# A state-space scan moved into the delta rule's scan, with batched 64-wide decays, in a one-core Trainium2 layer kernel

## What is computed

```python
def ssd_scan(x, bm, dt, A, s0, cm):            # per direction
    acum = cumsum(dt * A)                      # within a chunk of 64
    a_last = acum[..., -1]
    s_chunk = einsum('bgnsk,bghns,bghnsp->bghnkp', bm, exp(a_last - acum) * dt, x)
    def step(s, inp): sc, al = inp; return s * exp(al) + sc, s
    s_fin, s_starts = scan(step, s0, (s_chunk, a_last))
    seg = exp(where(c >= s, acum[c] - acum[s], -inf)) * dt[s]
    cb = einsum('bgnck,bgnsk->bgncs', cm, bm)
    y = einsum(cb, seg, x) + einsum(cm, s_starts) * exp(acum)
# then: y_f + y_b + D*x, times silu(z), rms_norm per group, joined with the delta output, @ w_out
```

## Time and profile before

| | |
|---|---|
| median of 3 runs | 1584.43 us |
| the profiled execution | 1585.72 us, span 1583.9 us |
| TensorE busy | 1329.1 us (84%) |
| VectorE, ScalarE, GpSimd busy | 505.1, 253.8, 124.0 us |
| DMA | 456.96 MB, mean 289 GB/s |
| stages by the timeline | delta 288.3 to 460.9, ssd 460.9 to 570.0 |

### The profile page before, as it was taken

How to read it: one execution, slowest core, us unless ns; L and a number is a source line. 1 busy time by engine, 2 the same in 40 slices (tenths; PEclk the granted TensorE clock), 3 DMA queues, 4 the chain that set the end, 5 groups by cost and what they waited for, 6 DMA issues and landing times.

```text
span 1583.9 us, 26942 instructions
## 1 busy us (share of the span) xinstructions
PE 1329.1 (84%) x11056; PEld 627.9 (40%) x11057; DVE 505.1 (32%) x1073; ACT 253.8 (16%) x450; POOL 124.0 (8%) x173
## 2 busy tenths in 40 slices
PE   5899899645657937999898898898899999999995
PEld 1746334535545423333333333333243333333332
DVE  0115333472455755232221321221131223232323
ACT  2411421104120131111110110110010001010102
POOL 1101220322115130000000000000000000000000
PEclk9599999755565867999999999999899999999998
DMA  9304255000031056999999999999999879997993
GB/s 369 140 13 138 88 208 205 2 4 4 3 130 38 0 242 275 426 429 427 427 429 427 428 427 429 427 427 427 427 428 427 382 320 428 428 413 300 427 427 144
DMA packets 46946, 456.96 MB, mean 289 GB/s; under 512 B 4227, under 2 KB 4483, under 8 KB 21795
## 3 DMA queue, kind: packets, MB, share of 16 engines
q1 hardware_dynamic: 46886, 456.08, 69.3%
HBM read 455.01 MB, written 1.05 MB: 288 GB/s over the span
## 4 chain that ended last, share of the span: by engine, by line
PE 33%; DMA 26%; DVE 2%; ACT 2%; issue 1%; DVEq 0%; ACTq 0%
DMA arena<-in_w_up 26%; PE bank L999 20%; PE bank L1028 8%; PE bank L971 2%; PE bank L962 2%; ACT arena L1302 1%; PE bank L992 1%; PE bank L1023 0%; DVE arena L1775 0%; ACT arena L1300 0%; DVE arena L1778 0%; ACT L1077 0%; ACT L1075 0%; DVE arena L1919 0%; DVE arena L1769 0%
## 5 line engine op out<-in xcount | busy, mean ns | idle before, releaser
L999 PE MATMUL bank<-arena 128*64 128x512 f32 x2176 | 483.5, 597 | 33.8 <-DMA arena<-in_w_up 19.1
L999 PEld LDWEIGHTS bank<-arena 128*64 128x64 f32 x2176 | 154.9, 137 | 343.7 <-issue 269.6
L1028 PE MATMUL bank<-arena 128*64 128x512 f32 x1088 | 239.4, 592 | 0.0
L1883 DVE TENSOR_SCALAR arena<-bank 128x512 f32<-128x512 f32 x34 | 23.6, 693 | 395.4 <-PE bank L999 395.4
L1028 PEld LDWEIGHTS bank<-arena 128*64 128x64 f32 x1088 | 78.5, 136 | 138.1 <-issue 135.7
L566 PE MATMUL bank<-arena 128*128 128x512 f32 (+1 forms) x320 | 119.0, 528 | 0.0
L1864 DVE TENSOR_TENSOR arena<-arena,bank 128x512 f32<-128x512 f32 x140 | 86.6, 681 | 6.0 <-PE bank L971 6.0
L566 PEld LDWEIGHTS bank<-arena 128*128 128x128 f32 x320 | 60.2, 189 | 55.9 <-issue 53.5
L962 PEld LDWEIGHTS bank<-arena 128*128 128x128 bf16 x1680 | 60.2, 118 | 27.0 <-DVE arena L1887 25.8
L971 PE MATMUL bank<-arena 64*128 64x512 f32 x280 | 69.6, 614 | 0.9 <-ACT arena L1304 0.9
L962 PE MATMUL bank<-arena 128*128 128x64 bf16 x1680 | 64.1, 199 | 1.1 <-DVE arena L1806 1.1
(11 more groups left out here) (331 smaller groups left out, 1226.8 us busy)
## 6 DMA issues: line engine op xcount, KB each, us to landing
arena<-in_w_gate SPq DMA_DIRECT2D x64, 2048.0 KB, 20.2
arena<-in_w_up SPq DMA_DIRECT2D x64, 2048.0 KB, 21.9
arena<-in_w_down SPq DMA_DIRECT2D x64, 2048.0 KB, 21.2
arena<-in_w_ada SPq DMA_DIRECT2D x12, 2048.0 KB, 9.4
arena<-in_wfm SPq DMA_DIRECT2D x20, 512.0 KB, 6.5
arena<-in_wz SPq DMA_DIRECT2D x2, 2048.0 KB, 20.1
arena<-in_w_out SPq DMA_DIRECT2D x1, 4096.0 KB, 17.9
arena<-in_x SPq DMA_DIRECT2D x2, 1024.0 KB, 10.9
```

The lines of the kernel that those rows point to most:

```text
L999: last = mm(ps[m][64 * c_:64 * c_ + 64, :], xcT[:, k, :], ring[:, 2 * h_ + m, k % 4, 512 * c_:512 * c_ + 512], start=False, stop=(k == KT ...
L1028: last = mm(ps[2][64 * c_:64 * c_ + 64, :], hidT[:, k % 4, 64 * (k // 4):64 * (k // 4) + 64], ring[:, 4 + h_, k % 4, 512 * c_:512 * c_ + 5 ...
L1883: v.tensor_scalar(hid[:, 0], ps[0][:, :], LIMIT, None, ALU.min).then_inc(*L.mark("a"))
```

## The change

Five things are done together.

1. **Decays dense.** The `ssd` decays are made per tile and direction (4 rounds G instead of 8) in 64x64 blocks, as those of the delta rule are: GpSimd prepares mask minus sum (`sNG`), TensorE 16 products of 64x64 (`ssd_decay`), VectorE one add of 512 columns (`ssd_rel`), ScalarE one exponential, VectorE one product with `cb` (`ssd_couple`), GpSimd one product with dt (`sM`). Rounds 0 and 1 stand ahead of `solved(1)`, 2 and 3 inside the scan.
2. **The state-space scan inside the delta scan.** The 14 input products (`ssd_input`), adds (`ssd_state`) and fades (`ssd_fade`) stand between the steps of the delta scan. The delta scan uses banks 0, 1 and 4, 5 only; the input products use banks 2 and 3. Four of the eight weighted inputs are made by ScalarE (32 operations of 64 columns), four by GpSimd.
3. **The rest of `ssd`.** It starts with `Y`. Tile 1 has banks of its own (0, 1, 7) and does not wait for VectorE's work on tile 0. The products within a chunk are 32 of 64x64 per tile instead of 8 of 128x128.
4. **The delta output is transposed out of `zs` directly**; the copy of it into `mix` (L2087) is gone.
5. **Places and loads.** `sM`, `xw`, `SS` lie in areas that the delta rule has left; `x` is loaded during `delta`; `wout` behind delta's barrier as before, now at the place of `US`; `wr` behind `Y` of tile 1.

```diff
 # TensorE, stage delta
+            def ssd_decay(G):
...
+                        last = mm(bk[r, 64 * head:64 * head + 64], gA[r, 2 + t, ch:ch + 1].broadcast_to([64, 64]),
+                                  tri[r, d, 64 * half:64 * half + 64], start=True, stop=True)
+            def ssd_input(n, d):
+                t, half = divmod(step_of(n, d), 2)
+                r = slice(64 * half, 64 * half + 64)
+                pe.wait_ge(*L.at("act" if t >= 2 else "pool", "xw", t, d))
+                if n:
+                    pe.wait_ge(*L.at("act" if n == 1 else "dve", "SS", n, d))
+                for g in range(2):
+                    last = mm(ps[2 + d][:, 256 * g:256 * g + 256], b_tm[r, t, 128 * g:128 * g + 128],
+                              xw[t // 2][r, t % 2, d, 4 * g:4 * g + 4, :], start=True, stop=True)
...
+            pe.wait_ge(*L.at("act", "XTd", 1))
+            pe.wait_ge(*L.at("dve", "XTd", 1))
+            ssd_decay(0)
+            ssd_decay(1)
+            ssd_gram()
             solved(1)
...
+                if n == 1:
+                    ssd_decay(3)
+                elif n == 2:
+                    ssd_input(1, 0)
+                    ssd_input(1, 1)
+                elif n >= 5:
+                    ssd_input(n - 2, 1)
...
+                if n == 0:
+                    ssd_decay(2)
+                    ssd_input(0, 0)
+                    ssd_input(0, 1)
+                elif n == 3:
+                    ssd_input(2, 0)
+                    ssd_input(2, 1)
+                elif n >= 4:
+                    ssd_input(n - 1, 0)
...
+                if t == 0:
+                    ssd_input(6, 0)
+                    ssd_input(6, 1)
 # TensorE, stage ssd
+                inter, intra = ((2, 3), 4) if t == 0 else ((0, 1), 7)
...
+            pe.wait_ge(*L.at("dve", "Y", 0))
             project(0, range(4))
...
+            pe.wait_ge(*L.at("dve", "Y", 1))
             project(1, range(KT)).then_inc(*L.mark("m", 1))
 # ScalarE
-            for b in range(2):
-                inverses(b)
-                solutions(b)
+            inverses(0)
+            solutions(0)
+            inverses(1)
+            ssd_decay(0)
+            ssd_decay(1)
+            solutions(1)
+            ssd_weigh(2, 0)
+            for d in range(2):
+                act.wait_ge(*L.at("pe", "BX", 0, d))
+                f(SSt[:, d], ps[2 + d][:, :], ACT.Copy).then_inc(*L.mark("SS", 1, d))
+            ssd_decay(2)
...
 # VectorE
+            for G in range(2):
+                ssd_rel(G)
+            for G in range(2):
+                ssd_couple(G)
...
+                if n in (2, 3):
+                    ssd_state(1, n - 2)
+                elif 4 <= n < 7:
+                    ssd_state(n - 2, 0)
...
+                if n < 2:
+                    ssd_rel(2 + n)
+                elif n < 4:
+                    ssd_couple(n)
+                else:
+                    ssd_state(n - 2, 1)
 # GpSimd
+            fades = {1: ((1, 0), (1, 1)), 2: ((2, 0),), 3: ((2, 1),), 4: ((3, 0),), 5: ((3, 1), (4, 0)),
+                     6: ((4, 1), (5, 0), (5, 1), (6, 0), (6, 1))}
 # SyncE
+                if st == "delta":
+                    sp.wait_ge(*L.at("pe", "scattered", 1))
+                    load("x", xin, x.rearrange("(t p) d -> p t d", p=P))
...
-            load("x", xin, x.rearrange("(t p) d -> p t d", p=P))
             load("wout", wout, w_out.rearrange("(k p) n -> p k n", p=P))
...
-            load("wr", area("wr"), w_router)
             L.stage("ssd")
+            sp.wait_ge(*L.at("pe", "Y", 1))
+            load("wr", area("wr"), w_router)
```

More of the change, by code:

```diff
@@ L1235, in _ @@
             L.stage("ssd")
-            for g in range(8):
-                act.wait_ge(*L.at("dve", "srel", g))
-                f(sDT[:, g % 2], sDT[:, g % 2], ACT.Exp).then_inc(*L.mark("sDT", g))
             def mixed_out(n, m, t):
@@ L2053, in _ @@
                 g_.tensor_tensor(view(Se[:, n % 2], 8, C), view(cur, 8, C), e_, ALU.mult).then_inc(*L.mark("Se", n))
+                for m, d in fades[n]:
+                    ssd_fade(m, d)
+            for G in range(4):
+                t, d = divmod(G, 2)
+                pool.wait_ge(*L.at("dve", "smt", G))
+                pool.wait_ge(*L.own())
+                g_.tensor_tensor(sM[:, G], sM[:, G], sp_[:, 2 + t, 16 + 8 * d:24 + 8 * d].unsqueeze(2).broadcast_to([P, H, C]), ALU.mult).then_inc(*L.mark("sM", G))
             pool.wait_ge(*L.own())
```

222 lines of the change are left out of this document (108 added, 114 removed).

## The result

| | before | after |
|---|---|---|
| median, run in turns on one chip | 1584.03 us (1582.88 to 1586.60, 4 runs) | 1532.66 us (1529.43 to 1534.80, 4 runs) |
| ratio | | 0.9673, 95% interval 0.9658 to 0.9688 |
| profiled execution, its span | 1585.72, 1583.9 us | 1529.43, 1527.6 us |
| expert weights issued | 570.03 us | 512.79 us |

The gain is 51.4 us; 48.5 were forecast, and 1532.66 lies inside the range. The profiled execution is the fastest of its four, so it shows some 3 us more than the median.

What follows compares the result with a forecast made beforehand. The expert loop leads, starting behind the barrier that ends `ssd`, so time removed ahead of it comes off the end one for one. Terms -44.3 - 2.6 + 1.3 - 1.9 - 1.0 = -48.5 us gave a 1536 us median, range 1531 to 1541.

Steps and rivals of the forecast that it cites:

- a: Decays and scan taken out of `ssd`, up to the first `Y` product: -44.3 us.
- b: From `Y` to the big projection, 28.4 us instead of 31.0: -2.6 us, ends -3.2 and -2.0.
- The cover of `wout`: Load ahead of the projection loses its 61 us of cover; landing estimated at 15.5 us, 1.6 us of slack, cost 0.
- rival 3: Tail waits for a load: `wout` or biases land 5 us later than estimated, +3.5, so 1540 us; chance 0.08.
- c: Behind the start of the projection, the same work, 22.5 us then 11.3 to the barrier: 0.
- d: Ahead of the delta scan, decay and Gram products before `solved(1)`: +1.3 us, ends 0 and +3.
- e: Inside the delta scan: +8.8 us at slow clock, -4.4 at fast; clock rise expected after two steps, -1.9 us.
- Rival 2: Matmuls run strictly in program order, so pairs of input products in the scan cost more: 1538 us; chance 0.06.
- Rival 1: TensorE's clock stays at 1.2 GHz in the scan, which then costs +8.8: 1548 us; chance 0.20.
- f: Delta outputs behind the scan, first group some 0.9 us shorter with the clock up: -1.0 us.
- Rival 4: The two scans' chains add up instead of interleaving, 3.7 us per input product: +23, 1608 us; chance 0.03.
- Rival 5: The earlier start is lost again in the expert loop, so no gain: about 1584 us; chance 0.03.

Runs made afterwards that it cites:

- again: The changed kernel run once more without an edit: 1533.67 us, ratio 0.9690 to the kernel before.
- wout_late: The changed kernel with a 2 MB load that nobody reads ahead of `wout` on SyncE's queue: 1541.14 us, ratio 0.9720 to the kernel before.
- bias_held: The changed kernel with VectorE's bias work held until GpSimd has made both mix tiles: 1535.61 us, ratio 0.9691 to the kernel before.
- best: The changed kernel with half of `w_out` loaded earlier, D*x products ahead of the wait for `Y`, bias casts held: 1532.91 us, ratio 0.9682 to the kernel before.
- fill_all: The kernel before with two idle near-zero products on one row half behind every WS and KV of the delta scan: 1599.16 us, ratio 1.0101.
- fill_data: The kernel before with one-row-half idle products behind every WS and KV, multiplying the delta rule's own numbers: median 1598.49 us, ratio 1.0041.

## Why the prediction was right

- **The start of the loop sets the end.** Right. The weights are issued 57.2 us earlier and the span is 56.3 shorter; in `again` 53.7 and 52.0. Two of the signs named in advance lie a little outside: from delta's barrier to the issue it is 59.4 us (`again` 59.8) and not 61 to 63, and the scan is 24.2 us (`again` 25.7) and not 25 to 27.
- **a, -44.3.** Exact, since it was read off.
- **b, -2.6, measured -3.8 and -3.4.** Outside the ends of the sum, -2.0 and -3.2. VectorE's work on a tile was 6.2 us as taken. The first `Y` ended at 5.6 us at a partly risen clock, where 6.9 at the slow one was assumed; that is the whole miss.
- **The cover of `wout`.** Forecast: landing in 15.5 us, 1.6 us of slack. It landed in 14.6 (`again`: 15.0), the quarter then took 9.9 us, begun at the low clock, instead of 8.7, and the slack was 0.5 (`again`: 0.3). `wout_late` shows that beyond it nearly every microsecond counts. So the mechanism of rival 3 exists, but what it wanted, a late landing, did not happen.
- **c, 0, measured -1.6.** This term was mis-sized. I took the projection over at 22.5 us; its first three microseconds had been at the low clock before (0.51 from 536 to 539). Now the first quarter runs just ahead of it, and it took 20.87 us in `again` and `bias_held` too. `best`, with a gap ahead of it, has 22.3 again.
- **d, +1.3, measured +1.6 and +3.0.** Inside its ends, in `again` at the upper one: there the clock rose at 406 only (0.54 from 403 to 406), in the first profile at 402 (0.96 from 402 to 404).
- **e, -1.9, measured -3.5 and -2.0.** The mechanism was right in kind: with the clock up from the start the scan is shorter than with the clock down in the first steps. The agreement of `again` with the forecast is luck, as two misses cancel. With the clock up throughout, the profiled scan comes out at -3.5, where -4.4 was the sum; and the slow start of `again` cost 1.5 us, where 2.5 was taken.
- **The price of an input product.** That a pair costs one slot and not two was right: 1.14 us against 1.13. The Trainium skill's rule of strict order (TensorE: Matmul & The Clock Gate, Part 3: Packing small matmuls), as the prediction worked it out, would have made a pair dearer than a lone product, and the run does not agree. Rival 2 falls. But the price itself was too low: 0.83 to 0.87 us at the fast clock, where one follows the other in 1.06 to 1.07 (412.25 to 413.32, 428.74 to 429.80), and 1.66 to 1.7 at the slow one, where it is 1.99 in `fill_all` (421.17 to 423.16). The cause is a misread row. The earlier trace rows were taken for the slow clock, but the clock rose inside them, at 484.8 of 482.32 to 485.63 (the columns are length, PE and PEld busy with L879, PEclk, DMA share, GB/s):

```profile
484.40:484.80 0.40, 0.40 (x5) 0.40 (x5) 0.50 0.00 0
484.80:485.20 0.40, 0.40 (x7) 0.40 (x4) 0.95 0.00 0
```

- **Rival 1 was priced too low** for the same reason: the scan of `fill_all`, with 14 lone fillers at the slow clock, takes 41.3 us, 13.6 more than before, where +8.8 was the sum of the rival.
- **The reason given for the clock.** Wrong as worded. The prediction expected a rise because the scan begins "with hardly a gap for 7 us". `fill_all` has no gap for 40 us and loses the clock. In the execution profiled first nothing had to rise in the scan: the clock had been at 1.00 since 404 and did not fall. Where it did fall (`again`), it rose under the decays and the pair, on both halves of the rows. So the forecast of a fast scan was right, for a reason that was half of the true one. That rival 1 had 0.20 was fair: with lone products alone (`fill_data`) 8 of 10 runs were in the group at 1596 us and above.
- **f, -1.0, measured -3.0.** Mis-sized, in both profiles alike. The outputs run wholly at 2.4 GHz: the first group takes 3.0 us (434.86 to 437.88) in place of 5.0, the second 3.0 (441.29 to 444.32) in place of 4.5, where -0.9 and "a little" were taken.
- **Rival 4** falls: no input product or state add waits for 1 us. (Its threshold of 3.4 us per product leaves out the 18 us that it adds for the decays; with them it is 46.9 less 18 over 14, 2.1 us.) **Rival 5** falls with the first point.

The terms b, c, e and f missed by -0.1 to -2.0 us each, d by +0.3 and +1.7. That the sum came out near has luck in it: these misses add up to -6.1 us in the first profile and -2.8 in `again`. The misses of b, c and f have one main cause: I priced the clock's rise for the scan alone, and it told on the delta outputs, `Y` and the projection as well.

## What to carry to other kernels

Two serial recurrences that each leave every engine idle behind a handoff can share the gaps: here 28 us for an order written by hand, with no engine made faster; put each foreign operation behind one whose operands are older. Price every stretch of TensorE at both clock levels and say which one the work ahead of it leaves, since a gap closed in one place can halve a duration in the next, and a gap opened by a faster neighbour takes it back (`best`). Before shortening one chain, see how far behind the second it ends: 0.3 us here, and `bias_held` gained 0.1.

## What was not expected of the hardware

- 40 us of TensorE without a pause, with two products at a time on one half of the rows, at 1.2 GHz (one profile, and the times of all 5 runs within 2.2 us); the same places filled on both halves, 2.4 GHz (one profile, and the times of all 10 runs in one group). Both scans began at 2.4 GHz.
- A kernel with two times, 1576 to 1581 and 1596 to 1601 us, in one and the same program (`fill_data`). The profile, of an execution of 1597.85 us, has its scan at 1.2 GHz; that the scan of the shorter two was at 2.4 is read from the time only.
- Useless products made the kernel before faster by 0.34% (interval 0.22 to 0.47).
- GpSimd's product of 128x512 took 1.27 us with VectorE idle, 1.33 beside a product of VectorE with one tensor as input (L1805), and 2.71 beside VectorE's cast to bf16 and the subtraction behind it.
